# Reordered loads, table loads, subtractions and the final combination in a two-layer mixed backbone kernel

## The reference, cut to what matters

```python
for l in range(DEPTH):                      # 2 layers
    mp, ms = modulation(c_ctx, ...), modulation(c, ...)   # shift, scale, gate, twice
    y = even_mixer(modulate(x, shift, scale)) if l % 2 == 0 else odd_mixer(...)
    x = layer_norm(ALPHA * x + gate * y) * g + b
    y = swiglu(modulate(x, ...)) if l % 2 == 0 else moe_swiglu(...)   # top 2 of 8 experts
    x = layer_norm(ALPHA * x + gate * y) * g + b
# even_mixer: u = h @ w_in; gated width-3 convolution and mean pooling; concat @ w_out
# moe_swiglu: y = sum over e of gates[e] * (silu(h @ wg[e]) * (h @ wu[e])) @ wd[e]
```

## Time and profile before

| | us |
|---|---|
| median of 3 runs | 1439.56 (1438.74 to 1440.28) |
| the profiled execution's own time | 1440.28 |
| span of its trace | 1438.3 |
| PE busy | 1372.1 (95%) |
| DVE busy | 858.3 (60%) |
| ACT busy | 650.5 (45%) |
| POOL busy | 113.4 (8%) |

### The profile page before, as it was taken

The page is one execution under the profiler, slowest core; times in us unless marked ns, Lnnn a source line. Parts: engine busy times, 40 slices in busy tenths (PEclk is TensorE's granted clock), DMA queues, the critical chain, the costliest instruction groups (busy, mean ns, idle before and its releaser), DMA issues.

```text
span 1438.3 us, 19348 instructions
## 1 busy us (share of the span) xinstructions
PE 1372.1 (95%) x6533; PEld 1077.9 (75%) x6534; DVE 858.3 (60%) x1122; ACT 650.5 (45%) x721; POOL 113.4 (8%) x119
## 2 busy tenths in 40 slices
PE   5999999999999998899999999999999999999994
PEld 2555469999999645555548888888888888888882
DVE  2102465324242433433337879888889898998987
ACT  0101043223242411222116567787777777777772
POOL 0500004000000330000000001001010000101000
PEclk8999999999999998998998999999999999999997
DMA  9976574524332823118007799999999999999993
GB/s 366 362 278 233 222 240 140 175 88 145 118 116 74 310 87 119 31 48 299 37 21 282 271 337 348 380 395 363 363 369 370 378 378 362 371 380 357 378 371 124
DMA packets 138793, 362.53 MB, mean 252 GB/s; under 512 B 14403, under 2 KB 48422, under 8 KB 138246
## 3 DMA queue, kind: packets, MB, share of 16 engines
q1 hardware_dynamic: 132512, 339.06, 63.7%
q0 software_dynamic: 5968, 22.91, 5.1%
q10 hardware_dynamic: 278, 0.10, 0.0%
HBM read 351.34 MB, written 10.68 MB: 252 GB/s over the span
## 4 chain that ended last, share of the span: by engine, by line
PE 84%; DVE 6%; DMA 5%; issue 3%; ACT 2%; SPq 0%; DVEq 0%; ACTq 0%
PE ps L1821 17%; PE ps L1823 17%; PE ps L1822 17%; PE ps L1786 6%; PE ps L1723 6%; DMA sb_expert_raw<-in_moe_w_up 3%; PE ps L1913 3%; PE ps L1683 2%; DVE sb_expert_w L1451 2%; PE ps L1657 1%; PE ps L2016 1%; DMA sb_ring<-in_ada_w 1%; PE ps L2012 1%; PE ps L1987 1%; PE ps L1998 1%
## 5 line engine op out<-in xcount | busy, mean ns | idle before, releaser
L1451 DVE TENSOR_TENSOR sb_expert_w<-sb_expert_raw,sb_expert_w 128x1792 fp32r<-128x1792 f32 (+1 forms) x300 | 479.8, 1648 | 49.1 <-ACT sb_expert_w L958 47.9
L958 ACT CAST sb_expert_w<-sb_expert_raw 128x1792 fp32r<-128x1792 f32 (+1 forms) x300 | 410.4, 1396 | 123.8 <-DMA sb_expert_raw<-in_moe_w_up 86.9
L1821 PE MATMUL ps<-sb_expert_w,sb_expert_x 128*128 128x448 f32 x640 | 238.8, 373 | 3.1 <-DVE sb_expert_x L1514 2.0
L1822 PE MATMUL ps<-sb_expert_w,sb_expert_x 128*128 128x448 f32 x640 | 236.1, 369 | 0.0
L1823 PE MATMUL ps<-sb_expert_w,sb_expert_x 128*128 128x448 f32 x640 | 236.0, 369 | 0.0
L1821 PEld LDWEIGHTS ps<-sb_expert_w,sb_expert_x 128*128 128x128 f32 x640 | 121.4, 190 | 15.4 <-DVE sb_expert_w L1451 3.1
L1823 PEld LDWEIGHTS ps<-sb_expert_w,sb_expert_x 128*128 128x128 f32 x640 | 121.3, 190 | 10.9
L1822 PEld LDWEIGHTS ps<-sb_expert_w,sb_expert_x 128*128 128x128 f32 x640 | 121.4, 190 | 10.0
L1821 PE MATMUL ps<-sb_split_acts,sb_split_weights 128*128 128x384 f32 x352 | 118.7, 337 | 0.4 <-issue 0.4
L1823 PE MATMUL ps<-sb_split_acts,sb_split_weights 128*128 128x384 f32 x352 | 118.7, 337 | 0.0
L1822 PE MATMUL ps<-sb_split_acts,sb_split_weights 128*128 128x384 f32 x352 | 118.5, 337 | 0.0
(11 more groups left out here) (282 smaller groups left out, 1765.7 us busy)
## 6 DMA issues: line engine op xcount, KB each, us to landing
sb_expert_raw<-in_moe_w_gate SPq DMA_DIRECT2D x160, 448.0 KB, 7.1
sb_expert_raw<-in_moe_w_up SPq DMA_DIRECT2D x160, 448.0 KB, 8.2
sb_expert_raw<-in_moe_w_down SPq DMA_DIRECT2D x140, 512.0 KB, 5.8
sb_ring<-in_ada_w SPq DMA_DIRECT2D x14, 3072.0 KB, 17.5
sb_ring<-in_ffn_w_gate SPq DMA_DIRECT2D x44, 256.0 KB, 3.7
sb_ring<-in_ffn_w_up SPq DMA_DIRECT2D x44, 256.0 KB, 4.8
sb_ring<-in_ffn_w_down SPq DMA_DIRECT2D x22, 512.0 KB, 6.2
sb_ring<-in_ev_w_in SPq DMA_DIRECT2D x4, 2048.0 KB, 14.9
```

The lines of the kernel that those rows point to most:

```text
L958: nc.scalar.copy(EWS[r][:, 0, 0:w], ERAW[:, r, 0:w]).then_inc(e_hi, 1)
L1451: V.tensor_tensor(EWS[r][:, 1, 0:w], ERAW[:, r, 0:w], EWS[r][:, 0, 0:w].bitcast(F32), ALU.subtract)\
L1821: first = mm(out, lh, rh, start=start, stop=False)
L1822: mm(out, lh, rl, start=False, stop=False)
```

## The change

Seven things are moved or taken out. Line numbers below are those of the kernel before, and its lines in the changed kernel differ by a few.

1. SP issues panel 1 ahead of both parts of `X`. PE transposes `X` after panel 1's product and turn, not ahead of them.
2. POOL's first three loads no longer wait for panel 2.
3. Both one-element square roots of ACT are gone. The table with the square root is now loaded at the first real root of each `squares` group, behind its first Square.
4. In the first item DVE makes five low parts ahead of `hidden(0)`, and `picked(1)` comes behind `hidden(0)`; before, three low parts and `picked(1)` stood ahead of it.
5. In the last half, four high and low parts stand ahead of `h_high` and `h_low`, not three, and `sums_room` comes behind the fourth low part.
6. `GB` is loaded by POOL, once DVE has split the last item's tokens (`xe_done`), and `LG` and `LB` after `sums_room`.
7. DVE does `before_last(0)`, then the gating of the last product, then `before_last(1)`, `summed(0)`, `before_last(2)`, `summed(1)`.

```diff
@@ SP
             ada(0)
+            ada(1)
             sp.dma_start(X[:, 0, :], x_prompt[0]).then_inc(x_in, 16)
             sp.dma_start(X[:, 1:NG, :], x_sample[0].rearrange("(g p) d -> p g d", p=P)).then_inc(x_in, 16)
-            ada(1)
             ada(2)
...
-            sp.wait_ge(stored, 16 * 2 * DEPTH)
-            sp.wait_ge(xe_done, more + 2)
-            sp.dma_start(GB[:, :, :], gate_rows[1, 2:4, :].partition_broadcast(P)).then_inc(gates_back, 16)
             sp.wait_ge(sums_room, 1)
@@ POOL
-            pool.wait_ge(landed[2], 16)
             pool.dma_start(PW, ev_pool_w[0].rearrange("g c d -> c g d")).then_inc(pw_in, 16)
...
-            pool.wait_ge(y_got[NG - 1], 16)
+            pool.wait_ge(gate_passed, more * 2 + 1)
+            pool.wait_ge(xe_done, more + 2)
+            passed()
+            pool.wait_ge(stored, 16 * 2 * DEPTH)
+            pool.dma_start(GB[:, :, :], gate_rows[1, 2:4, :].partition_broadcast(P)).then_inc(gates_back, 16)
+            pool.wait_ge(sums_room, 1)
@@ ACT
             high(FF_LAST, FF_LAST_USED)
-            nc.scalar.activation(SM[:, 23:24], cst("eps"), ACT.Sqrt)
             ada_stage(10)
...
-            for c in range(3):
+            for c in range(4):
                 expert_high(e_last(more, c), "d")
             h_high(more * 2 + 1)
-            for c in range(3, EB):
+            for c in range(4, EB):
                 expert_high(e_last(more, c), "d")
-            nc.scalar.activation(SM[:, 23:24], cst("eps"), ACT.Sqrt)
@@ DVE
-            expert_lows(None, FIRST_KINDS, 7, KD + 2)
+            expert_lows(None, FIRST_KINDS, 7, KD + 4)
+            hidden(0)
             picked(1)
-            hidden(0)
-            expert_lows(None, FIRST_KINDS, KD + 2, KD + 3)
+            expert_lows(None, FIRST_KINDS, KD + 4, KD + 5)
             h_low(0)
-            expert_lows(None, FIRST_KINDS, KD + 3, KD + 5)
...
-            for c in range(3):
+            for c in range(4):
                 expert_low(e_last(more, c), "d")
             V.tensor_copy(ROWW[:, 2, :], ROWW[:, 1, :]).then_inc(sums_room, 1)
             h_low(more * 2 + 1)
-            expert_low(e_last(more, 3), "d")
...
-            for g in range(NG):
-                before_last(g)
+            before_last(0)
             dve.wait_ge(yd, more + 1)
             for v in range(2):
                 V.scalar_tensor_tensor(YV[:, v, :], ...).then_inc(y_gated, 1)
+            before_last(1)
...
             summed(0)
+            before_last(2)
             summed(1)
@@ PE
             ada_mm(0)
-            pe.wait_ge(st_a, 1)
-            x_turned(0)
             ada_mm(1, None, 0)
             ada_turn(1, True)
+            x_turned(0)
             ada_mm(2)
```

## The result

The changed kernel took 1448.69 us (median of 5, 1445.63 to 1449.13) against 1438.74 (1436.47 to 1440.28, 5) for the kernel before: ratio 1.0069, 95% interval 1.0052 to 1.0086. Timed again later with its parts, it took 1445.75 against 1440.86: 1.0044 (1.0026 to 1.0062). (A ratio is worked out from all runs of both kernels and is not quite the quotient of the two medians.) It is slower, as forecast. The first timing puts it at 9.9 us (7.5 to 12.4), the second at 6.3 us (3.7 to 8.9), where I had worked out 5.0. The profiled execution has a span of 1447.1 us (before 1438.3), 8.8 more.

A forecast was written before the change was run, and what follows sets the result against it. PE was taken to bound the kernel, with DVE carrying the last 20 us. Terms 2.8 + 0.1 + 3.9 - 1.8 = +5.0 us on the median 1439.56 gave 1444.6 us, range 1441.7 to 1446.5 for 8 in 10.

The forecast's parts named there:

- start: Up to the first input projection: POOL's early loads make the first input weights land later, at 42.0 us; +2.8 us.
- table loads: SwiGLU's normalisation and program end: the load behind the first Square delays the root DVE reads; +0.1 us in all.
- first item: First expert item: PE's transposes wait for two more low parts of 1.93 us each; +3.9 us, bounds 0 and 4.5.
- `GB`, `LG`, `LB`, fourth part: Last half: moved loads and fourth high and low part cost nothing, as ACT's idle 3.69 us fits a 1.05 us cast.
- first item to last transposes: Expert stage: PE sets the pace, so the earlier delay is not made up there; 0 us.
- interleave: End: gating starts with PE's last product, two `before_last` fill DVE's waits, 21.8 us to the end; -1.8 us.
- clock rival: Start: PE at 1.2 GHz through transposes and product holds the projection until 43.7 us; +1.7, time 1446.3 us; chance 8%.
- That rival (-3.9 us): Expert stage: the first item's delay is made up because the weight stream sets the pace; time 1440.7 us; chance 7%.
- The condition that I wrote myself: End: if `GB` sharing DMA made the fourth piece over 2.6 us later, `h_high` would be late; bounds 0 and +1.5.

The follow-up runs named there:

- only-item: Kernel before with only DVE's new first-item order (five low halves and hidden product ahead of the pick): 1443.62 us against 1440.86, ratio 1.0027.
- only-gate-loads: Kernel before with only the `GB`, `LG` and `LB` loads moved to POOL's earlier place, three parts ahead of `h_high`: 1441.75 us against 1439.99, ratio 1.0016.

## Why the prediction was half right

The start, the table loads and the first item came out near the forecast; two terms at the end did not. The first timing's 1448.69 us lie 2.2 us above my range of 1441.7 to 1446.5; the second timing, 6.3 us above 1438.74, would be 1445.0 and lies inside it. By parts, with the first profile beside it, and each timed on the kernel before (ratio times 1438.7):

| term | forecast | profile | timed alone |
|---|---|---|---|
| start | +2.8 | +3.15 | +4.2 (1.9 to 6.5) |
| table loads | +0.1 | +0.1 | not timed |
| first item | +3.9 | +3.65 | +3.9 (2.3 to 5.6) |
| `GB`, `LG`, `LB`, fourth part | 0 | +2.05, and 0 in the second profile | +1.7 (0.3 to 3.0) |
| last down product partly at half clock | none | +1.6 | in no part's account |
| first item to last transposes | 0 | +0.5 | in no part's account |
| interleave | -1.8 | -2.15, not all its own | -0.4 (-1.7 to +0.9) |
| sum | +5.0 | +8.8, then +5.9 | +9.4, plus or minus 3.4 |

**Start.** Right in mechanism and near in size: full DMA engines pass POOL's megabyte on to the first input weights. The clock rival did not decide: PE waited 0.96 us for the weights. My account did not allow for the noise of this stretch: from 39.0 to 41.3 us in kernels that are equal here. Before's 39.19 was one of the early ones. The means are 40.1 and 42.8 us, 2.6 apart, which is close to the 2.8 of the forecast; timed alone the start is 1.4 us above it, within its interval.

**First item.** Right, two low halves. PE was the bound behind it, and nothing was made up. That rival (-3.9 us) is refuted by only-item, whose interval starts at 2.3 us.

**Moving `GB` and the fourth part.** This is the first step that failed: "I cost these at nothing". It measured 2.05 us of wait on PE in the first profile, and 1.7 us (0.3 to 3.0) timed alone. The condition that I wrote myself, a fourth piece over 2.6 us late, came true in the profile. I had counted ScalarE's 3.69 us of idle time as cover for a 1.05 us cast, and cover for the cast is not cover for the landing. The cast began 4.18 us into that idle time, 0.72 us after `h_high` could have started. With its own 0.95 us it made `h_high` 1.67 us late, and VectorE's low half ahead of `h_low` added 0.39 us. `GB`'s megabyte at 364 GB/s is 2.9 us by itself. That the piece was late because of `GB` is argued from the order of issue: with `GB` ahead of it, its cast began 6.6 to 8.3 us after its issue in three of eight profiles, and with four parts ahead and `GB` behind, 3.4 and 4.6 us after it in the two profiles there are. The early gate loads cost 2.3 us (0.3 to 4.3) without the four parts too, and for that I have no row: only-gate-loads' profile is one of its short executions.

**The interleave.** The second term that was mis-sized, by some 1.2 to 1.4 us: forecast -1.8, timed alone -0.4, and -0.6 by the means of the profiles. The mechanism came about: the gating starts 0.04 us after the product, and gating to end takes 21.6 us (forecast 21.8). The comparison was wrong. I sized the gain against one execution, and its 23.8 us are the longest of ten endings in the old order. The waits that I meant to fill were 2.74 + 1.14 us there and 0.95 + 0.29 to 2.75 + 1.54 in the other nine. Where the product itself is late, the three rows fit beside it and the new order is the longer one. That the first profile shows a gain of 2.15 us, near the forecast, is luck: it depends on which execution of the kernel before was profiled. The timing alone can't exclude a gain of up to 1.7 us.

**The rest.** Half clock in the last down product had no term in my sum. It gave 1.6 us in this pair of profiles, but it comes and goes in kernels of all orders, so these runs don't show it as a cost of the change. By the parts timed alone, my sum was short by 1.7 us at the gate loads and fourth part, 1.4 us at the interleave and 1.4 us at the start; only the first of the three is clear of the noise. The 0.5 us that the first timing has above the sum of the parts is within the noise too.

What stays open: why the early gate loads cost something when three parts are ahead, where the panel order's cost arises, and whether the difference between 1.0069 and 1.0044 for the same kernel is more than how often the fourth piece is late.

## What to carry to other kernels

Before an operation is put in front of one on the path, ask what it waits for: idle time of the engine covers its duration, not the arrival of its data. Ask as well what the same change does to that arrival. When a gain is read as a wait that is to be filled, look at the granted clock of the rows on both sides of the wait and at more than one execution, for a wait that comes from half-clock products may be shorter in the next. And turn a harmful reordering round once: the item's new order added 3.65 us of wait, its opposite took 1.4 away.

## What the runs showed that I had not expected

The granted clock falls to 0.50 (1.2 GHz) for 3.4 us in the last down product, which costs PE 1.6 us of work, and for up to 20.5 us at a time elsewhere. With the same 2.20 us wait before it, the last down product took 9.9 us in seven profiles and 11.5 us in eight, over all orders. The combining products were more regular: after PE had been idle for 1.47 or 1.70 us they ran at full clock in 5.39 us (eight profiles), and after 2.12 to 4.64 us partly at 0.50, in 6.95 to 8.43 us (ten profiles). The interleave shortens that idle time, so part of what it gains may come by way of the clock. Over the profiles of this study such stretches took 31 to 41 us of PE's time, and executions of one kernel on one chip lay 3 to 16 us apart. A single pair of profiles can't tell a 2 us effect here, though from the first projection to the SwiGLU's end, where the clock is the same, the two traces agree to 0.13 us (448.95 and 449.08).
